# Stage A's weights in whole rows, the first loads spread over two queues, no copy of x, and other orders in stage C's first chunks and at the MLP's change of phase

## The reference

```python
h = _rmsnorm(x, norm1_g[l]);  z = h @ w_in[l]            # 1024 x 1024 @ 1024 x 2824
mq, mk, mv, mi, mf, mo, aq, ak, av = jnp.split(z, split_idx, axis=-1)
qk = jax.nn.silu(_causal_dwconv(concat([mq, mk]), conv_w[l], conv_b[l]))
hm = _mlstm_chunkwise(mq, mk, mv, mi + bias, mf + bias)  # 4 heads of 128, a recurrence over chunks
hm = _rmsnorm(hm, mlstm_norm_g[l]) * jax.nn.sigmoid(mo)
ha = _swa_sinks(_rope(_rmsnorm(aq, q_norm_g[l])), _rope(_rmsnorm(ak, k_norm_g[l])), av, sinks[l])
x = x + jnp.concatenate([hm, ha], axis=-1) @ w_out[l]
h2 = _rmsnorm(x, norm2_g[l])
x = x + jnp.square(jax.nn.relu(h2 @ w_ff1[l])) @ w_ff2[l]   # width 4096
```

## Time and profile before

| | before |
|---|---|
| runs | 2226.62 us median of 3 (2225.19 to 2227.73) |
| profiled execution, its own time | 2224.22 us |
| its span | 2222.4 us, so 1.8 us lie around it |
| PE busy | 2119.3 us (95%) |
| DVE, POOL, ACT busy | 1410.7, 977.5, 852.3 us |
| DMA | 427.31 MB in 237585 packets |
| PE's idle time in the first 38 us | 34.35 us (38.00 less 3.65 busy) |

### The profile page before, as it was taken

How to read it: one execution, slowest core, us unless ns; L and a number is a source line. 1 busy time by engine, 2 the same in 40 slices (tenths; PEclk the granted TensorE clock), 3 DMA queues, 4 the chain that set the end, 5 groups by cost and what they waited for, 6 DMA issues and landing times.

```text
span 2222.4 us, 32528 instructions
## 1 busy us (share of the span) xinstructions
PE 2119.3 (95%) x10964; PEld 1757.7 (79%) x10964; DVE 1410.7 (63%) x1674; ACT 852.3 (38%) x1427; POOL 977.5 (44%) x695
## 2 busy tenths in 40 slices
PE   3999997999999999999989999889999999999998
PEld 3888876888788877788888888778878887778886
DVE  3127775457777787667550388644767777866764
ACT  3224433336666642212241343432656666221210
POOL 3234424333455554545442356143244555454542
PEclk9999999999999999999999999999999999999999
DMA  7224225424676688876642223344166667987673
GB/s 246 69 87 131 68 79 171 152 85 163 239 239 236 238 307 305 318 291 264 237 126 90 95 76 103 116 155 152 57 218 229 235 238 238 359 313 281 271 274 142
DMA packets 237585, 427.31 MB, mean 192 GB/s; under 512 B 31272, under 2 KB 175400, under 8 KB 229168
## 3 DMA queue, kind: packets, MB, share of 16 engines
q1 hardware_dynamic: 224560, 402.92, 51.4%
q10 hardware_dynamic: 12928, 23.14, 2.9%
HBM read 272.77 MB, written 157.42 MB: 194 GB/s over the span
## 4 chain that ended last, share of the span: by engine, by line
PE 59%; issue 19%; POOL 12%; DVE 5%; DMA 2%; SPq 1%; ACT 1%; DVEq 0%; ACTq 0%; POOLq 0%
PE ps L1804 20%; PE ps L1525 10%; PE ps L1456 9%; POOL w1s L1375 8%; PE ps L1615 7%; PE ps L1434 4%; POOL w2s L1379 3%; PE ps L1756 1%; DMA gB<-in_norm_g 1%; DMA uk<-uD 1%; PE ps L1425 1%; PE ps L1549 1%; PE ps L1576 1%; PE ps L1563 1%; PE ps L1660 1%
## 5 line engine op out<-in xcount | busy, mean ns | idle before, releaser
L1804 PE MATMUL ps<-w2s,uk 128*128 128x512 f32 x2688 | 618.6, 392 | 7.4 <-DVE uf L2353 3.9
L1804 PEld LDWEIGHTS ps<-w2s,uk 128*128 128x128 f32 x2688 | 504.9, 189 | 120.1 <-issue 11.5
L2317 DVE TENSOR_TENSOR xs<-ps,xs 128x1024 f32<-128x1024 f32 x208 | 253.3, 1221 | 172.0 <-PE ps L1804 170.2
L1756 PE MATMUL ps<-hT,w1s 128*128 128x512 f32 x1344 | 319.4, 393 | 11.0 <-DVE uf L2279 5.2
L1756 PEld LDWEIGHTS ps<-hT,w1s 128*128 128x128 f32 x1344 | 251.2, 189 | 74.2 <-issue 12.5
L1379 POOL TENSOR_TENSOR w2s<-raw,w2s 128x1024 fp32r<-128x1024 f32 x64 | 182.8, 2878 | 180.5 <-ACT w2s L1157 180.5
L1375 POOL TENSOR_TENSOR w1s<-rawf,w1s 128x512 fp32r<-128x512 f32 x112 | 167.0, 1503 | 198.7 <-ACT w1s L1051 198.7
L1525 PE MATMUL ps<-hT,whi 128*128 128x512 f32 x768 | 244.1, 399 | 0.0
L1756 PE MATMUL ps<-tT,w1s 128*128 128x512 f32 x1008 | 237.3, 389 | 0.0
L1756 PEld LDWEIGHTS ps<-tT,w1s 128*128 128x128 f32 x1008 | 189.1, 188 | 39.5 <-issue 0.4
L1456 PE MATMUL ps<-ahi,hT 128*128 128x512 f32 (+1 forms) x768 | 209.5, 357 | 2.9 <-DVE hT L1852 2.9
(11 more groups left out here) (209 smaller groups left out, 3144.6 us busy)
## 6 DMA issues: line engine op xcount, KB each, us to landing
uk<-uD SPq DMA_DIRECT2D x64, 1024.0 KB, 8.8
raw<-in_wstream SPq DMA_DIRECT2D x104, 512.0 KB, 6.1
uk<-uD SPq DMA_DIRECT2D x64, 768.0 KB, 7.7
rawf<-in_wstream SPq DMA_DIRECT2D x64, 512.0 KB, 4.3
uD<-uh SPq DMA_DIRECT2D x64, 512.0 KB, 5.1
uD<-uf SPq DMA_DIRECT2D x64, 512.0 KB, 5.3
uD<-uh SPq DMA_DIRECT2D x64, 384.0 KB, 4.2
uD<-uf SPq DMA_DIRECT2D x64, 384.0 KB, 5.2
```

The costliest lines, as they stand in the source:

```text
L1756: mm = pe.matmul(ps[:, bank, :], w, x[:, k, :], start=(first and k == 0 and i == 0), stop=(k == 3 and i == 2), skip_group_check=True)
L1804: mm = pe.matmul(ps[:, bank + tp, :], u, w2s[r][:, w, k, :], start=(r in (1, 2, 5) and k == 0 and i == 0), stop=(k == 1 and i == 2), skip_ ...
L2317: V.tensor_tensor(y, ps[:, bank:bank + 2, :], y, ALU.add).then_inc(y_acc, 1)
```

## The change

There are five parts.

1. **Loads at the start.** Stage A's ten units are ten whole slabs of `wtoken` (128 rows of 4128 bytes, one DMA each) in place of 24 pieces. Since a slab has 258 columns and the groups are 264, 512 and 512 wide, unit 1's split first takes 6 more columns for group 0 out of units 2 and 3, and unit 5's takes 2 more for group 1 out of units 6 and 7 (`ahead`), on ACT and on POOL. SP loads the gain gB right behind the identity, then four units, then tiles 3 to 7 of x; ACT loads x's tiles 0 to 2 alone. The mask and the triangle come last. `zD`'s columns lie in order, so that group 0's result is one DMA a tile, not two.
2. **No copy of x to the output.** ACT's eight DRAM-to-DRAM copies are gone; layer 1's residual is read from x.
3. **Stage C's first chunks.** Chunk 0's numerator waits for one memset less; the scores of chunk 1 are issued in chunk 0; `lo_out(3)` moves from POOL to DVE, `lo_out(7)` and `lo_out(5)` move within DVE's list; on POOL `lo_out(4)`, the mask of chunk 2 and `lo_out(6)` come ahead of `mix_lo(0, 0)`; on ACT the splits of k = 3 to 6 come ahead of `mix_hi(0, 0)`.
4. **Last block of phase 1.** Product 1 runs ahead of product 2.
5. **Phase 2.** The sums for r = 6 and r = 7 change places, both in general and at the change of phase; SP loads the first half of uk for g = 2 ahead of w2 of g = 2.

The diff, cut to its core:

```diff
-                def piece(g, kh, k0, ks, c0, dst):
...
+                sp.dma_start(raw[slot][:], wtoken[l, n]).then_inc(s_raw[slot], 16)
...
                 if l == 0:
-                    unit_a(l, 0, 0)
                     sp.dma_start(gB[:], norm_g[l, 0].partition_broadcast(P)).then_inc(s_gain, 16)
-                    unit_a(l, 1, 1)
+                    for n in range(4):
+                        unit_a(l, n, n)
+                    for t in range(3, NT):
+                        sp.dma_start(xs[:, t, :], x_t[t]).then_inc(s_x[t], 16)
                     load_par(l)
-                    unit_a(l, 2, 2)
-                    unit_a(l, 3, 3)
+                    sp.dma_start(maskf[:], consts[2]).then_inc(s_mask, 16)
+                    sp.dma_start(tri[:], consts[1]).then_inc(s_mask, 16)
...
+        BLOCK = ((0, 0, 0, 258), (1, 0, 6, 252), (1, 252, 0, 258), (2, 0, 2, 256), (2, 256, 0, 256))
+        MORE = {1: (0, 258, 0, 6), 3: (1, 510, 0, 2)}
+        def ahead(n):
+            return {1: (2, 3), 5: (6, 7)}.get(n, ())
...
             def split_a(l, n):
-                landed(act, l, n % RING, 2 * (n // RING) + (1 if n < 6 else 2), 0)
-                nc.scalar.copy(unit_hi(n), unit_raw(n)).then_inc(w_hi, 1)
+                for m in ahead(n):
+                    landed(act, l, m % RING, m // RING, 0)
+                    nc.scalar.copy(unit_in(m, ahi, True), unit_raw(m, True))
+                landed(act, l, n % RING, n // RING, 0)
+                nc.scalar.copy(unit_in(n, ahi), unit_raw(n)).then_inc(w_hi, 1)
...
-            act.dma_start(xs[:, 0, :], x_t[0]).then_inc(s_x[0], 16)
-            for t in range(1, NT):
+            for t in range(3):
                 act.dma_start(xs[:, t, :], x_t[t]).then_inc(s_x[t], 16)
-            for t in range(NT):
-                act.dma_start(out_t[t], x_t[t]).then_inc(s_spill, 16)
+            act.sem_inc(s_spill, 16 * NT)
...
-                split_out(3)
-                mix_hi(0, 0); att_hi(0, 1)
-                split_out(4); split_out(5)
+                for k in range(3, 7):
+                    split_out(k)
+                mix_hi(0, 0)
+                split_out(7)
+                att_hi(0, 1)
                 squares(0, 1)
-                split_out(6); split_out(7)
...
-                pool.wait_ge(c_hn, l * NT + 1)
-                lo_out(3)
-                mix_lo(0, 0); att_lo(0, 1)
                 lo_out(4)
+                masked(1, 0)
+                lo_out(6)
+                mix_lo(0, 0)
                 scale_c(0, 1)
...
-                for r, bank, first in ((2, 0, True), (1, 4, True), ...
+                for r, bank, first in ((1, 4, True), (2, 0, True), ...
...
-                w2_sum(0, 1); w2_sum(0, 2)
+                w2_sum(0, 1)
                 dve.wait_ge(f_m, FZ + POSZ[3] + 1)
                 V.tensor_tensor(u[:, A21, :], ps[:, 6, :], u[:, A12, :], ALU.add).then_inc(f_w, 1)
                 dve.wait_ge(f_w, AZ + 6)
                 V.tensor_tensor(u[:, A12, :], ps[:, 7, :], u[:, 1, :], ALU.add).then_inc(f_w, 1)
-                w2_sum(0, 3)
+                w2_sum(0, 2); w2_sum(0, 3)
...
+                load_u(2, 0, 0, 14 + 4)
+                load_u(2, 0, 1, 14 + 7)
                 sp.wait_ge(m2_lo, l * (7 * GR) + 14)
                 alone(sp)
                 load_w2(2)
                 store_u(LAST, 1)
-                for b in range(2):
-                    load_u(2, b, 0, 14 + (7 * b + 4))
-                    load_u(2, b, 1, 14 + (7 * b + 7))
+                load_u(2, 1, 0, 14 + 7 + 4)
+                load_u(2, 1, 1, 14 + 7 + 7)
```

More of the change, by code:

```diff
@@ L32 @@
 ZW = 5 * GW
-GC = (264, 512, 512)
-ZX = ZV + 512 - 6
+GC, G0 = (264, 512, 512), (0, 264, 776)
 ROWP = 64 + 64 + 8 + 8
@@ L83, in trunk_kernel @@
         ring_r = Region(qk_r.at)
-        raw = [ring_r(f"raw{s}", [P, 4 * GC[0]], F32) for s in range(RING)]
+        raw = [ring_r(f"raw{s}", [P, 4 * GW], F32) for s in range(RING)]
+        ring_r.at = fixed.at + (ring_r.at - fixed.at + 511) // 512 * 512
         hilo_at = ring_r.at
@@ L1264, in unit_a @@
                     pool.wait_ge(w_hi, l * U + (n + 1))
-                    nc.gpsimd.tensor_tensor(unit_lo(n), unit_raw(n), unit_hi(n).bitcast(F32), ALU.subtract).then_inc(w_lo, 1)
+                    for m in ahead(n):
+                        nc.gpsimd.tensor_tensor(unit_in(m, alo, True), unit_raw(m, True), unit_in(m, ahi, True).bitcast(F32), ALU.subtract)
+                    nc.gpsimd.tensor_tensor(unit_in(n, alo), unit_raw(n), unit_in(n, ahi).bitcast(F32), ALU.subtract).then_inc(w_lo, 1)
                 if l == 0:
@@ L1366, in _ @@
                 barrier(pool, p_pool, (p_pe, p_sp, p_dve, p_act), l * PHASES + 1)
-                for _ in range(5):
+                for _ in range(6):
                     pool.sem_inc(w_lo, 1)
@@ L1645, in step_c @@
                             project(T - 1, 1 - p, 0, False, True)
-                    if not first:
-                        pe.wait_ge(c_qe, T - l)
                     pe.wait_ge(c_wd, T + 1)
                     pe.wait_ge(c_in[p], (l * 4 + j) * 32 + 32)
-                    pe.wait_ge(c_one, l * 3 + 3)
+                    pe.wait_ge(c_one, l * 3 + (2 if first else 3))
                     if not first:
@@ L2095, in step_c @@
                         V.tensor_copy(scl[:].unsqueeze(2), erB[p][:, :, P - 1:P]).then_inc(c_scl, 1)
-                        V.tensor_tensor(qe[:], erB[p], qkT[:, i, 0:MH, :], ALU.mult).then_inc(c_qe, 1)
+                        V.tensor_tensor(qe[:], erB[p], qkT[:, i, 0:MH, :], ALU.mult)
                         weights(i, T, last)
+                    if second:
+                        lo_out(5)
                     if not (first or second):
@@ L2113, in step_c @@
                     elif second:
-                        lo_out(5)
+                        lo_out(7)
                     dve.wait_ge(c_den, T * 7 + 5)
@@ L2135, in step_c @@
                     if first:
-                        lo_out(2)
-                    if second:
-                        lo_out(7)
+                        lo_out(2); lo_out(3)
                     dve.wait_ge(c_ht, T + 1)
```

113 lines of the change are left out of this document (43 added, 70 removed).

## The result

| | before | changed |
|---|---|---|
| median of the runs | 2226.59 us (2225.19 to 2227.73, 4 runs) | 2207.67 us (2206.57 to 2208.19, 4 runs) |
| profiled execution, its span | 2224.22, 2222.4 us | 2208.19, 2206.4 us |
| PE, DVE, ACT, POOL busy | 2119.3, 1410.7, 852.3, 977.5 us | 2119.6, 1402.9, 856.1, 983.1 us |
| DMA | 427.31 MB, 237585 packets | 423.13 MB, 222801 packets |

The ratio is 0.9914, 95% interval 0.9903 to 0.9926. The forecast was 2210 us, 2199 to 2219. The busy times hardly moved; what went is idle time of PE.

The account below looks back on a forecast made before the run. PE, busy 2119.3 of 2222.4 us, was the bound, leaving idle time and half-clock stretches to win. Terms -18.5 - 1.5 - 3 + 6.5 = -16.5 gave 2207.7 profiled, 2210 us median (chance 0.52), range 2199 to 2219.

Parts of the forecast that it names:

- The start, -18.5: Stage A's start: first matmul at 19.1 us in place of 37.66, gain 18.5 us, bounds 13 to 21.
- that SP's packets are small: Start loads: queues take turns by packet, so gB behind SP's small packets lets ACT's large ones pass; 26.4 us to land.
- the first paragraph: The bound: PE's 33.36 us idle at the start, a third of all idle time, because DVE's scaling waits for gB.
- The whole rows: Unit loads in rows of 4128 bytes: priced at no more than the pieces, even if cut at 4096.
- Layer 2's stage A, -1.5: ACT's second zD issue a tile goes, which once kept PE idle 1.63 us: 1.5 us gained, between 0 and 4.
- Stage C, -3 for both layers: Chunk 1: one 6 us wait for the mixed heads' lo part replaces two; 3 us gained, bounds 0 and 9.
- The change of phase, +6.5: MLP: w2 of g = 2 lands late behind uk, a hole near 6 us; loss 3.3 a layer, 6.5 in two.
- the gains are swallowed because DVE is bound: Change of phase: DVE has no less to do; it loses 2.9 to 4 us a layer in spite of its gains.
- A: Rival: w2's late load is hidden or the change of phase gains as meant; about 2200 us, chance 0.24.
- D: Rival: w2 stays late through phase 2, the hole returning in five later g, some 4 us each; 2250 us, chance 0.02.
- B: Rival: the start gains less, PE held to 24 us, and stage C's half-clock hole takes its gain; 2220 us, chance 0.19.
- C: Rival: gB lands late again because SP's queue still takes turns with ACT's; about 2230 us, chance 0.03.

Follow-up runs that it names:

- zd_two: The changed kernel with group 0's stage A result stored by two DMAs a tile (258 and 6 columns), as before: 2212.33 us.
- copies_back: The changed kernel with ACT's eight copies of x to the output issued again behind its loads of x: 2220.26 us.
- before_start_pieces: The kernel before with the new start (gain first, four units, x tiles on SP, no copies) but units still in pieces: 2205.04 us.
- before_gain_first: The kernel before with the gain gB loaded ahead of unit 0, nothing else: 2225.72 us, ratio 0.9997 to before.
- c_mix_first: The changed kernel with the mixed heads' lo part first on POOL and their hi part right behind k = 3's split on ACT: 2201.52 us.
- old_orders: The changed kernel with w2 of g = 2 and the stores ahead of uk, and old orders of last-block products and w2 sums: 2200.34 us.
- w2_first: The changed kernel with w2 of g = 2 and the last hidden block's stores ahead of uk's loads on SP: 2192.47 us.

## Why the prediction was right, and where it was not

The total is 2.3 us from the forecast, but that is in part luck. The forecast's sum, 2207.7, was for the profiled execution, which took 2208.19, so the steps add up to -16.0 where I had -16.5. In this sum layer 2's stage A gained 3.1 us more than forecast, while the change of phase lost 1.9 more and layer 1's phase 1 1.6 that I had not foreseen: they cancel. The 2.4 us that I added for the median lying above the profiled execution held for the kernel before and not for the changed one, whose median lies 0.5 us below it.

- **The start, -18.5, measured -18.6.** The first part of the chain came as worked out: gB at 7.76 us, unit 3 at 14.5 (I had 13.5), two small copies of 0.21 us, POOL's 2.19 us in place of 2.85, the first matmul at 18.51 (19.1). What follows it did not: for PE's own start at the lower clock I had 0.7 us and it cost 2.7, and the 2.1 us that group 0 gained behind it, about 1.6 of them from the second zD issue (zd_two), I had put at nothing in layer 1. These two errors nearly cancel, so the size of this term is luck in part. The turns by packet are shown by the equal counts in the earlier trace rows and in copies_back, and copies_back moves the first matmul by 12.5 us. What I had put first, that SP's packets are small, is wrong as a cause on its own (before_start_pieces): it is large packets on the other queue that hold small ones. And gB's landing, the one releaser that I built the first paragraph on, was worth nothing by itself (before_gain_first). The 0.7 us for the completion of a load, like the 1.5 and 1.3 us to start and complete at the change of phase, came from no row.

**The whole rows.** I priced them at no more than the pieces. The Trainium skill, DMA: Bandwidth & Descriptors, prefers packets of at most 4096 bytes (SWDGE vs HWDGE vs iDMA, in its table on transfers issued from GpSimd; these loads are SP's). The trace bears no cost out. The DMA of the changed kernel from 2 to 14 us has 143 packets under 512 bytes, where four units cut at 4096 would have added some 500 rests of 32:

```profile
DMA packets 1320, 4.49 MB, mean 374 GB/s; under 512 B 143, under 2 KB 241, under 8 KB 1320
```

The Trainium skill, DMA: Bandwidth & Descriptors (Specifications), also asks for transfers of at least 512 bytes for line rate. The rate of before_start_pieces, whose pieces are of 1032 and 24 bytes, agrees (333 GB/s against 418 from 8 to 16 us), but no run separates the two sizes, and it cost no start.

- **Layer 2's stage A, -1.5, measured -4.6.** Mis-sized. I took one wait of 1.63 us from the earlier trace rows and let the others count as unchanged, though PE waited 5.0 us for y in that stretch. The second issue is 2.0 us of it (zd_two); the 2.18 us wait behind the slow scaling went as well, which I had not looked at, and it stays open what took it away.
- **Stage C, -3 for both layers, measured -2.4 and -0.5.** Right in place, releaser and size. PE was ready at 334.7, 353.3 in the times of the kernel before (I had 353.3), the wait was 7.5 us and not 6, and the end is 367.9, the case with the clock at its lower level, for which I had 368.5. c_mix_first shows that this order gives away 3 us a layer.
- **The change of phase, +6.5, measured +8.4** (the four steps of the table, -2.7 + 7.8 - 4.2 + 7.5). Product 20 ended 2.5 us earlier against the block before (2.4 forecast) in layer 1 and DVE had w2 12.7 us behind it (12). Mis-sized is what follows the hole: I let the last products end at 897 with a lower clock, 27.6 us behind product 20; it was 29.1, with 10.2 us at clock 0.51 and product 24 taking 5.3 us in place of 2.72. In layer 2 w2 took 1.2 us longer. That "the gains are swallowed because DVE is bound" fell: they are kept (old_orders), 7.9 us.
- **Not foreseen: +1.6 us in layer 1's phase 1.** The same wait for DVE's uf stands there in both kernels (2.19 and 2.18 us), followed by a stretch at clock 0.55 in the changed one and none before. It is not the change's: before_gain_first, which is the kernel before up to one load at the start, has the stretch too, with a wait of 2.19 us, and so has every other kernel measured here. It is the profiled execution of the kernel before that lacks it. What decides it from one execution to the next stays open. Windows of before and of before_gain_first at this place:

```profile
563.70:567.10 3.40, 3.38 (x15) 2.81 (x16) 3.32 (x3) 2.26 (x2) 0.00 (x0) 1.00 1.02 374
562.50:565.90 3.40, 3.36 (x8) 2.71 (x9) 3.29 (x3) 2.25 (x3) 0.00 (x0) 0.50 1.01 371
```

- **The rivals.** A (2200) and D (2250) had the right place: w2's order decides. A's time of 2200 is passed with w2_first's order, 2192; D's hole does not repeat. B's condition (start later than 24 us) and C's (gB late) did not come.

## What to carry to other kernels

A load that waits for a product must not stand in the same queue ahead of one that could go at once: two lines on SP cost 15 us here, and the mended order with the mixed heads first is the version to take, 2183.9 us, 42.6 under the kernel before. Before believing the one releaser that a long idle time names, look at when the other inputs were ready; here one was ready only 1 us before. A copy that nobody waits for can be the dearest transfer of a start, if its packets are larger than those that are waited for.
